# Summing a head's squares in the retention: two GpSimd additions and one all-ones matmul in place of four matmuls

## The reference, cut to what matters

```
def _rms(x):
    xf = x.astype(jnp.float32)
    return xf * lax.rsqrt(jnp.mean(xf * xf, axis=-1, keepdims=True) + NORM_EPS)

def retention_mixer(h, w_in, w_out):
    q, k, v, gate = _split(h @ w_in, RET_IN_SIZES)
    ...
    o = _chunk_retention(q, k, v.reshape(b, t, C_HEADS, C_V_DIM))
    o = _rms(o).astype(h.dtype).reshape(b, t, C_V_WIDTH)
    return (jax.nn.silu(gate) * o) @ w_out
```

## Time and profile before

| | us |
|---|---|
| median of 3 runs | 3094.54 |
| range of the runs | 3093.50 to 3094.64 |
| profiled execution | 3094.47 |
| its span, first to last instruction | 3092.7 |
| TensorE busy | 3024.6 (98%) |
| VectorE busy | 1723.1 (56%) |
| ScalarE busy | 1349.7 (44%) |
| GpSimd busy | 202.7 (7%) |

### The profile page before, as it was taken

How to read it: one execution, slowest core, us unless ns; L and a number is a source line. 1 busy time by engine, 2 the same in 40 slices (tenths; PEclk the granted TensorE clock), 3 DMA queues, 4 the chain that set the end, 5 groups by cost and what they waited for, 6 DMA issues and landing times.

```text
span 3092.7 us, 62832 instructions
## 1 busy us (share of the span) xinstructions
PE 3024.6 (98%) x24215; PEld 2959.1 (96%) x24215; DVE 1723.1 (56%) x2483; ACT 1349.7 (44%) x1955; POOL 202.7 (7%) x222
## 2 busy tenths in 40 slices
PE   8899999999999999999999999999999999999997
PEld 7879999989999999999999999999999999999997
DVE  4787675465554455545555454554456554455545
ACT  4455454453343333334444444444344444344443
POOL 0011110020000000001100000000010000000002
PEclk9999999999999999999999999999999999999999
DMA  5213222434445544444444444444444455554553
GB/s 187 97 60 113 85 102 91 149 122 170 173 161 179 186 166 174 171 168 166 153 156 157 153 159 163 150 162 163 183 157 162 179 189 175 192 189 179 185 179 137
DMA packets 77503, 482.52 MB, mean 156 GB/s; under 512 B 8933, under 2 KB 11365, under 8 KB 32624
## 3 DMA queue, kind: packets, MB, share of 16 engines
q1 hardware_dynamic: 77360, 481.21, 43.8%
q0 software_dynamic: 64, 0.21, 0.0%
HBM read 479.29 MB, written 2.10 MB: 156 GB/s over the span
## 4 chain that ended last, share of the span: by engine, by line
PE 92%; DVE 5%; ACT 2%; issue 1%; DMA 0%; POOL 0%; DVEq 0%; POOLq 0%; ACTq 0%; SPq 0%
PE ps L443 91%; DVE w_lo L1664 1%; DVE w_lo L1760 0%; DVE x_lo L1711 0%; DVE bias L1883 0%; DVE u L1716 0%; PE ps L1031 0%; ACT w_hi L1099 0%; DVE conv_acc L1789 0%; DVE r_post L1674 0%; PE ps L653 0%; POOL h L2381 0%; DVE kq L1796 0%; DMA raw<-in_w_latent 0%; DVE bias L1897 0%
## 5 line engine op out<-in xcount | busy, mean ns | idle before, releaser
L443 PE MATMUL ps<-x_hi,w_hi 128*128 128x272 f32 (+1 forms) x4992 | 1459.8, 292 | 15.3 <-DVE w_lo L1664 11.7
L443 PE MATMUL ps<-x_lo,w_hi 128*128 128x272 f32 (+1 forms) x4992 | 1429.8, 286 | 10.7 <-DVE x_lo L1711 10.7
L443 PE MATMUL ps<-x_hi,w_lo 128*128 128x272 f32 (+1 forms) x4992 | 1426.6, 286 | 0.0
L1664 DVE TENSOR_TENSOR w_lo<-raw,w_hi 128x1024 fp32r<-128x1024 f32 (+2 forms) x952 | 1031.8, 1124 | 368.6 <-ACT w_hi L1099 354.7
L1099 ACT ACTIVATE w_hi<-raw 128x1024 fp32r<-128x1024 f32 (+1 forms) x902 | 848.7, 973 | 497.3 <-PE ps L443 404.0
L443 PEld LDWEIGHTS ps<-x_hi,w_hi 128*128 128x128 f32 x4992 | 942.8, 189 | 35.1 <-issue 25.2
L443 PEld LDWEIGHTS ps<-x_lo,w_hi 128*128 128x128 f32 x4992 | 941.0, 189 | 19.3 <-DVE x_lo L1711 16.0
L443 PEld LDWEIGHTS ps<-x_hi,w_lo 128*128 128x128 f32 x4992 | 943.2, 189 | 0.7
L443 PE MATMUL ps<-mid_hi,w_lo 128*128 128x256 f32 (+1 forms) x1920 | 546.4, 285 | 0.0
L443 PE MATMUL ps<-mid_hi,w_hi 128*128 128x256 f32 (+1 forms) x1920 | 546.1, 284 | 0.0
L443 PE MATMUL ps<-mid_lo,w_hi 128*128 128x256 f32 (+1 forms) x1920 | 545.1, 284 | 0.0
(11 more groups left out here) (249 smaller groups left out, 2275.2 us busy)
## 6 DMA issues: line engine op xcount, KB each, us to landing
raw<-in_w_up SPq DMA_DIRECT2D x176, 1024.0 KB, 4.8
raw<-in_w_ret_in SPq DMA_DIRECT2D x96, 1024.0 KB, 4.8
raw<-in_w_down SPq DMA_DIRECT2D x128, 704.0 KB, 4.0
raw<-in_w_heads SPq DMA_DIRECT2D x32, 1024.0 KB, 4.8
raw<-in_w_ret_out SPq DMA_DIRECT2D x32, 1024.0 KB, 4.8
raw<-in_w_mix_early SPq DMA_DIRECT2D x16, 768.0 KB, 4.3
raw<-in_w_latent SPq DMA_DIRECT2D x8, 1024.0 KB, 4.9
raw<-in_w_dsa SPq DMA_DIRECT2D x16, 256.0 KB, 2.6
```

The costliest lines, as they stand in the source:

```text
L443: return nc.tensor.matmul(o, lhs, rhs, start=start, stop=stop)
L1664: V.tensor_tensor(w_lo[:, slot, cut], raw[:, slot, cut], w_hi[:, slot, cut], ALU.subtract).then_inc(lo_ready, count)
```

## The change

GpSimd gets two additions in each head, behind the rotation of the key: the first waits for the squares and adds chunks 2 and 3 to chunks 0 and 1 (128 partitions x 512 numbers), the second waits for the first and adds chunk 1 to chunk 0 (128 x 256). TensorE waits for the second addition in place of the squares, and runs one all-ones matmul on chunk 0.

```
-        RG = Steps(sem("ret_pool"), "q k")
+        RG = Steps(sem("ret_pool"), "q k pair sum")
...
-                pe.wait_ge(RA.sem, RA.after("osq", i))
-                for j in range(4):
-                    last = mm(ps[:, BK_2, 0:SEQ], ones[:], ret_sq[:, j], j == 0, j == 3)
-                last.then_inc(RP.sem, 1)
+                pe.wait_ge(RG.sem, RG.after("sum", i))
+                mm(ps[:, BK_2, 0:SEQ], ones[:], ret_sq[:, 0], True, True).then_inc(RP.sem, 1)
...
                     G.tensor_tensor(dst[:, 0], rot_a[:, 0, t0:T], dst[:, 0], ALU.subtract)
                     G.tensor_tensor(dst[:, 1], rot_a[:, 1, t0:T], dst[:, 1], ALU.add).then_inc(RG.sem, 1)
+                pool.wait_ge(RA.sem, RA.after("osq", i))
+                G.tensor_tensor(ret_sq[:, 0:2], ret_sq[:, 0:2], ret_sq[:, 2:4], ALU.add).then_inc(RG.sem, 1)
+                pool.wait_ge(RG.sem, RG.after("pair", i))
+                G.tensor_tensor(ret_sq[:, 0], ret_sq[:, 0], ret_sq[:, 1], ALU.add).then_inc(RG.sem, 1)
```

## The result

| | before | changed |
|---|---|---|
| median, us | 3094.54 (7 runs, 3090.87 to 3097.55) | 3082.96 (7 runs, 3081.16 to 3084.57) |
| profiled execution's span, us | 3092.7 | 3082.8 |
| a head's period in the trace, us | 80.21 | 78.91 |

The ratio is 0.9962, with a 95% interval of 0.9953 to 0.9972: 11.6 us less, between 8.7 and 14.5. The forecast was 10.4 us less, 3084.1 us. Single runs lie up to 6.7 us apart (kernel before) and 3.4 us (changed), so the trace is the finer scale. The period is the distance of the first from the eighth head's squares, by seven: (2104.1 - 1542.6) / 7 before, (2094.8 - 1542.4) / 7 after. Lines of VectorE and ScalarE in the changed kernel stand two lower than before.

A forecast was written before the change was run, and what follows sets the result against it. TensorE, busy 98% of 3092.7 us, was taken to bound the kernel. Dropping 24 matmuls of 0.433 us saves 10.4 us, with the additions hidden by tile 10: 3094.47 - 10.4 = 3084.1 us, range 3082.0 to 3087.5.

The forecast's parts named there:

- TensorE bounds the retention: Retention heads: TensorE is busy 79.9 to 80.0 of 80 us, so work leaving its queue shortens the time.
- 0.433 us a matmul, 24 of them: Matmuls on ret_sq: three dropped in each of 8 heads, priced by distance of starts, 10.4 us less.
- 1.3 us for the unseen width: GpSimd's first addition, 128x512, a width not in the trace: estimated at 1.3 us, ends 0.74 and 1.54.
- Ready 2.0 us ahead: Sum of head 0: GpSimd's additions end with signals at 1546.2, 2.0 us before TensorE comes at 1548.21.
- An idle VectorE leaves the low price: GpSimd's additions lie in VectorE's 7.73 us idle gap, so 256 columns cost 0.740 us, not 1.718.
- What is late next: nothing, with 1.17 us to spare: Behind the sum: VectorE's drain of tile 11 comes 1.30 us earlier, still 1.17 us after the reciprocal's end.
- Rival 1: At the sum: GpSimd ends after tile 10, TensorE waits 1.05 us a head, 3092.5 us; chance 5%.
- rival 3: At the sum: second addition falls into VectorE's splits, TensorE waits 3.7 us a head, 3113.7 us; chance 3%.
- Rival 2: At the next head's tile 2: seven of eight heads give their gain back, 3093.2 us; chance 6%.

The follow-up runs named there:

- E1: Changed kernel without GpSimd's two additions, one all-ones matmul on the first chunk of squares, behind ScalarE's squares: 3082.34 us, ratio 0.9959 to the kernel before.
- E2: Changed kernel with GpSimd's two additions and TensorE's wait for them, but all four matmuls kept: 3094.58 us, ratio 0.9999 to the kernel before.
- E9: Changed kernel with two more chained 128x512 GpSimd additions of two distinct inputs ahead of the last addition: 3087.71 us, ratio 0.9981 to the kernel before.
- E10: Changed kernel with three more chained 128x512 GpSimd additions of two distinct inputs ahead of the last addition: 3109.30 us, ratio 1.0047 to the kernel before.
- E4: Changed kernel with three more chained 128x512 GpSimd additions of a tile to itself ahead of the last addition: 3091.88 us, ratio 0.9992 to the kernel before.
- E7: Changed kernel with VectorE's step mid_lo moved behind the drain of tile 0 in heads 1 to 7: 3080.94 us, ratio 0.9961 to the kernel before.
- E8: The changed kernel measured again, no edit: 3082.32 us, ratio 0.9960 to the kernel before.
- E5: Changed kernel with the two additions on VectorE in its idle stretch in place of GpSimd: 3081.30 us, ratio 0.9963 to the kernel before.
- E3: Changed kernel with two more chained 128x512 GpSimd additions of a tile to itself ahead of the last addition: 3084.14 us, ratio 0.9964 to the kernel before.

## Why the prediction was right

- **TensorE bounds the retention.** Right: E1 and E2 split the change into its halves, and all the time goes with the matmuls.
- **0.433 us a matmul, 24 of them.** Right: the period fell by 1.30 us. The four differences of run medians that belong to three dropped matmuls (10.7 to 12.0 us) all lie somewhat above 10.4, inside their intervals; what they have beyond it stays open. Counting starts and not lengths mattered: the lengths would have given 18.2 us. The span fell by 9.9 us and not 10.4: the first squares came 0.2 us earlier, and from the last squares to the end passed 988.6 us before and 988.0 after, where one head's 1.3 us would have been due. That 0.7 us does not come from a head's period.
- **1.3 us for the unseen width.** Right: 1.287. From two widths 16 columns apart the slope gave 0.0021 us a column, and from 256 to 512 columns it is (1.287 - 0.739) / 256 = 0.0021. That the two agree so closely is partly luck: the first was read from a difference of 0.03 to 0.04 us between rounded durations, and 0.0019 to 0.0025 would have fitted, 1.23 to 1.38 us for the addition.
- **Ready 2.0 us ahead.** Right in kind, a little short: the signals took 0.08 us (1543.45 to 1543.53, and 1544.82 to 1544.90) where rows of other places had 0.16 and 0.24, and in E9 TensorE started 0.06 us behind the last addition where 0.12 was taken. The cover measured by E9 is 2.37 us. It is one number of this place, 2.4 us of GpSimd time a head.
- **An idle VectorE leaves the low price.** Right, and E10 shows the other side. The rule of the Trainium skill that was weighed (SBUF — State Buffer, Who interferes with whom) holds here in both directions: in E10 the addition waits for a half of `w_lo` (1.58 us in place of 0.74), and in E4 the pair of `w_lo` waits for the addition (2.59 in place of 2.35).
- **What is late next: nothing, with 1.17 us to spare.** Right: VectorE's idle time before the drain is 1.13 us. The chain kept its length.
- **Rival 1** (GpSimd late) and **rival 3** (second addition beside the split) did not happen, but both exist: E9 and E10 make them. Rival 3's price was put at 3.7 us of wait and 3113.7 us, on the thought that the addition is held through both halves; it slips in between them. E10 waits 2.57 us and comes to 3109.3 us, part of it by TensorE's clock (last section). Rival 3's point of decision also has to be read more finely: it is when the last addition starts, not how long the first takes. **Rival 2** (given back at tile 2) falls with the equal lengths of the chain, and E7 shows that this place was worth only 0.35 us a head.

## What to carry to other kernels

On an engine that is busy all the time, price a removed instruction by the distance between starts, and check with a period in the trace, which here repeated within 0.02 us in 80 (E1, E2, E8 and E5 against the two kernels) where whole runs scatter by several us. Before handing work to another engine, look for the stretch in which it ends before the bound engine arrives and in which the engine that it takes turns with is idle: here there were 2.4 us of cover and 7.7 us of idle VectorE. Three more additions (4.1 us), of which the last fell beside VectorE's split, turned a gain of 0.4% into a loss of 0.5%. Once the work is covered, a faster engine for it brings nothing (E5).

## What was not expected of the hardware

**A short wait can cost TensorE's clock.** After the wait of E10, matmuls in head 0 start 0.21 us apart and not 0.12 (1550.56, 1550.74, then 0.21 each until about 1554). Busy time by stretch behind the sums of heads 0 and 5 of E10, which start at 1549.91 and 1960.79 (the first row names the columns, PEclk is the granted clock):

```profile
core 0: us, PE busy (x) PEld busy (x) DVE busy (x) ACT busy (x) POOL busy (x), PEclk, DMA share, GB/s
1549.90:1554.00 4.10, 4.09 (x20) 4.04 (x21) 2.79 (x2) 2.06 (x3) 0.00 (x0) 0.59 0.45 134
1961.00:1965.00 4.00, 4.00 (x34) 3.95 (x34) 2.57 (x2) 1.83 (x3) 0.00 (x0) 1.00 0.53 152
```

The granted clock of the first stretch is 0.59, mostly the 1.2 GHz level, with 20 matmuls; in head 5 it stayed at 1.00, with 34, after the same idle time on GpSimd (2.42 us, and 2.41 in head 0). Three of the eight heads show the drop (0, 1 and 6). What it costs can be read from one sum to the next: 82.97, 83.05 and 83.10 us where the first of the two heads has the drop, 81.61 to 81.63 in the four others. That is about 1.4 us a drop, 0.6 us a head on average, and without it the period is what the wait leaves to expect: 78.91 + 2.57 + 0.1 = 81.6. After the waits of E4 (1.0 us) and E9 (0.4 us) the clock stayed at 1.00. Why one head drops and the next does not, at the same wait, stays open; E10's trace is one execution.

**GpSimd adds a tile to itself faster than two tiles.** 1.04 us in place of 1.29 for 128x512 (E3 against E9, at the same place). What makes the difference was not tried further; for an experiment that stretches a chain it means that the dummy must read what the real one reads.
